# One layer of a hybrid decoder on one core: a norm's mean and two of its tiles given to other engines, and the first expert's transposes placed ahead of the loops

## Chip, cores, metric

The kernel runs on one core of a Trainium2 chip. The metric is the device time of one execution in microseconds (us), the median of several runs; less is better. The engines are named as in the profile: PE (TensorE), DVE (VectorE), ACT (ScalarE), POOL (GpSimd), SP (SyncE, which here only issues DMAs).

## What is computed

1024 tokens of width 1024, float32. The last of three sublayers is a mixture of 32 experts, top 4, and after it stands a final RMSNorm. The change lies in these two:

```
def moe_ffn(hn, ...):                       # hn = rmsnorm(h, ln_ffn)
    logits = xt @ w_router + b_router
    top_vals, top_idx = lax.top_k(logits, TOP_K); gates = softmax(top_vals)
    ... rows sorted by expert ...
    h = ragged_dot(xs, w_gate_up, sizes) + b_gate_up[e]
    act = glu * sigmoid(1.702 * glu) * (lin + 1)      # clamped
    y = (ragged_dot(act, w_down, sizes) + b_down[e]) * gates
    return segment_sum(y, tok)
...
h = h + moe_ffn(...)
return rmsnorm(h, ln_final)                 # h * rsqrt(mean(h*h) + eps) * ln_final
```

## The kernel before

Mixers, cross attention and router fill the first 1085 us of the profile. Then 32 experts ("items") run one after the other, sorted by how many rows they hold; the code exists once for each of six widths (256, 208, 184, 160, 144, 128 rows), the widest first. In this data the width of 256 holds no expert, the others hold 2, 2, 3, 6 and 19.

**The loops on PE.** For each width `up_to` nests five loops of two turns, each with an `If` on a register `at` that counts experts (L1916, L1917), and in the innermost stands `item(w)`. In it `If_lt(at, 1)` (L1909) guards `e_turn_in(0, range(4))`: the 16 transposes (L1760) that turn the first expert's gathered rows `xg`; for the 31 others they were made by the expert before. DVE copies them to `xe_t` (`x_copies`), and on that semaphore (`e_xt`) the first gate and up matmuls wait (L1376).

**The end.** All of the last expert but its own rows is summed in `d_sum` before it runs its down product. SP loads `d_sum` back as eight tiles `h_out` of 128 x 1024 (L603), and the final norm of these tiles runs beside the last matmuls:

- ACT squares and sums each tile (`squares`, L1311, semaphore `r_ss`).
- DVE makes the mean of a group of tiles (`means`, L2372, `f_mean`). The groups are F_TILES: tiles 0 and 1, tiles 2 to 5, tiles 6 and 7.
- POOL raises it to -0.5 (L1021, `f_rstd`).
- DVE multiplies a tile by its factor and by the weights `g_fin` in one instruction (`normed`, L2431), SP writes the tile to the output (L795, `f_out`).

In between DVE adds the last expert's rows (`last_rows`, two halves, `completed`, L2452), ACT squares those (L1353), DVE norms them too (`y_sb`), and POOL scatters them into the output (L1030). That scatter overwrites rows, so it waits for all eight tile writes.

ACT's last `step` has, after the squares, this loop; PE's last down product releases it piece by piece, the last piece (`e_dn[1]`, its second count) with the matmul that adds the bias (L1844):

```
for m in range(KD):
    b, k = (m // 2) % 2, m // 4 + 1
    if m % 2 == 0:
        ac.wait_ge(e_dn[b].full, 2 * i + k)
    if last:
        ...
        continue
```

Each engine carries out its own instructions in the order in which they are written.

Of the kernel before, what the change touches and what calls it, by code (L numbers as in the profile page):

```python
# [26 lines left out]
ALU = mybir.AluOpType  # L27
ACT = mybir.ActivationFunctionType
AX = mybir.AxisListType.X

P = 128
# [47 lines left out]
def build(nc, S, a, out):  # L79
    T, D, NT, KD, H, FW, E, CAP = S.T, S.D, S.NT, S.KD, S.H, S.FW, S.E, S.CAP  # L80
    ctx = ExitStack()
    with ctx:
# [38 lines left out]
        half = keep("half", [P, 16])  # L121
# [173 lines left out]
        h_out = Region(15, 47)("h_out", [P, NT, D])  # L295
        last_rows = Region(59, 63)("last_rows", [P, D])
        g_fin = r("g_fin", [P, D])
# [6 lines left out]
        rstd_f = r("rstd_f", [P, NT])  # L304
# [274 lines left out]
        s_st, r_gate = sem("s_st"), sem("r_gate")  # L579
# [3 lines left out]
        f_rstd, f_o, f_out = sem("f_rstd"), sem("f_o"), sem("f_out")  # L583
        f_mean, f_mean_done = a_latn, NT
        F_TILES = [(0, 2), (2, 6), (6, 8)]
        assert F_TILES[-1][1] == NT

        def apart(eng):
# [12 lines left out]
        def _(sp):  # L601
# [186 lines left out]
            def rows_for_norm():  # L788
                for t in range(NT):
                    load(h_out[:, t, :], d_sum[t * P:(t + 1) * P, :], f_in[t])  # L790

            def normed_rows(first):
                for t in range(NT):
                    sp.wait_ge(f_o, first + t + 1)
                    sp.dma_start(out[0, t * P:(t + 1) * P, :], h_out[:, t, :]).then_inc(f_out, 16)  # L795

            sp.wait_ge(e_left, E)
            rows_for_norm()
            normed_rows(0)

            def whole_norm():
                rows_for_norm()
                normed_rows(NT + 1)
                sp.wait_ge(f_out, 16 * 2 * NT)

            sp.wait_ge(f_out, 16 * NT)
# [4 lines left out]
        def _(po):  # L811
# [204 lines left out]
                bounds_check=T - 1, oob_is_err=False).then_inc(e_share, 16)  # L1016

            def norm_factors(first):
                for n, (t0, t1) in enumerate(F_TILES):
                    po.wait_ge(f_mean, f_mean_done + first + n + 1)  # L1020
                    po.tensor_tensor(rstd_f[:, t0:t1], rstd_f[:, t0:t1], half[:, 0:t1 - t0], ALU.pow).then_inc(f_rstd, 1)  # L1021

            norm_factors(0)
            po.wait_ge(f_mean, f_mean_done + len(F_TILES) + 1)
            po.tensor_tensor(rstd_l[:, 1:2], rstd_l[:, 1:2], half[:, 0:1], ALU.pow).then_inc(f_rstd, 1)
            further = any_further(po)
            po.wait_ge(f_out, 16 * NT)
            po.wait_ge(f_o, NT + 1)
            apart(po)
            po.indirect_dma_start(  # L1030
                out=out[0], out_offset=bass.IndirectOffsetOnAxis(ap=sidx[:, 0:1], axis=0),
# [24 lines left out]
        def _(ac):  # L1056
# [257 lines left out]
            def step(i, e, before, first=False, last=False):  # L1314
                for m in range(KD):
                    ac.wait_ge(e_glu, KD * i + m + 1)
                    ac.activation(sig[m % 2][:, :], glu[m % 2][:, :], ACT.Sigmoid, scale=1.702).then_inc(e_sig, 1)  # L1317
                    if m == 1 and before is not None:
                        rows_back(before)
                    if m == 1 and first:  # L1320
                        nothing_back()
                    if last and m >= 6:
                        squares(((0, 1), (2, 3, 4, 5, 6, 7))[m - 6], 2)
# [5 lines that stand above are left out]
                        if m % 2 == 1:  # L1329
                            ac.sem_inc(e_dn[b].free, 1)  # L1330
                        if m % 4 == 3:
                            ac.sem_inc(e_w[4 + m // 4].free, 1)
                        continue
                    x = ac.activation(y_t[:, m, :], pp2[b][:, (m % 2) * CAP:(m % 2 + 1) * CAP], ACT.Identity,  # L1334
                                      bias=b_dn[:, bass.ds(e * KD + m, 1)])
                    if m % 2 == 1:
                        x.then_inc(e_dn[b].free, 1)
                    if m % 4 == 3:
                        ac.sem_inc(e_w[4 + m // 4].free, 1)
                ac.drain().then_inc(e_yt, 1)  # L1340

            def expert_at(i):
                return ac.value_load(items[0:1, 0, bass.ds(i, 1)], min_val=0, max_val=E - 1)
# [4 lines left out]
            with ac.Fori(1, E - 1) as i:  # L1348
                step(i, expert_at(i), i - 1)
            step(E - 1, expert_at(E - 1), E - 2, last=True)  # L1350
            for b in range(2):
                ac.wait_ge(e_rows[b].free, rows_use(b, E - 1, 1) + 1)
                ac.activation(y_sb[:, 1, b * 512:(b + 1) * 512], last_rows[:, b * 512:(b + 1) * 512], ACT.Square,  # L1353
                              accum_out=sum_l[:, b:b + 1])
                ac.drain().then_inc(r_ss, 1)
# [9 lines left out]
        def _(pe):  # L1365
# [523 lines left out]
            for b in range(2):  # L1889
                pe.wait_ge(e_rows[b].free, e_rows[b].base + 1)  # L1890
                for m in range(4 * b, 4 * b + 4):
                    x = pe.transpose(wide[1][0:BP, m * P:(m + 1) * P],
                                     b_thrice[:, m, :], ident)
                x.then_inc(e_rows[b].full, 1)
            at = pe.alloc_register("item_at")
            pe.reg_mov(at, 0)
            LEVELS = 5
# [2 lines left out]
            def item(w):  # L1900
                i, n, n_before = pe.snap(at), pe.snap(held), pe.snap(held_before)
                later = pe.snap(held_later)

                def look_ahead():
                    pe.reg_mov(held_before, n)
                    pe.reg_mov(held, later)
                    pe.reg_mov(held_later, rows_in(i + 2))

                with pe.If_lt(at, 1):  # L1909
                    e_turn_in(0, range(4))  # L1910
                whole(i, i - 1, w, n_before, later, look_ahead)
                pe.reg_mov(at, i + 1)

# [21 lines left out]
        def _(ve):  # L1935
# [432 lines left out]
            def means(n, squared):  # L2368

                t0, t1 = F_TILES[n]  # L2370
                ve.wait_ge(r_ss, squared + t1)
                ve.tensor_scalar(rstd_f[:, t0:t1], sum_f[:, t0:t1], 1.0 / D, EPS, ALU.mult, ALU.add)  # L2372
                ve.drain().then_inc(f_mean, 1)
# [58 lines left out]
                ve.drain().then_inc(f_o, 1)  # L2432

            def norm(first, squared, between=None):
                for n, (t0, t1) in enumerate(F_TILES):
                    for t in range(t0, t1):
                        if between is None and t == 0:
                            means(0, squared)
                        if t == t1 - 2 and n + 1 < len(F_TILES):
                            means(n + 1, squared)  # L2440
                        ve.wait_ge(f_rstd, first + n + 1)
                        if between is not None:
                            between(t)
                        normed(h_out[:, t, :], h_out[:, t, :], rstd_f[:, t:t + 1])
# [8 lines left out]
                                        op0=ALU.mult, op1=ALU.add).then_inc(e_rows[b].free, 1)  # L2453

            def at_tile(t):
                if t == 3:
                    completed(0)
                elif t == NT - 1:
                    ve.wait_ge(r_ss, 2 * NT + 1)
                    ve.tensor_scalar(rstd_l[:, 0:1], sum_l[:, 0:1], 1.0 / D, EPS, ALU.mult, ALU.add)  # L2460
                    completed(1)
# [66 lines left out]
```

## Time and profile before

| | us |
|---|---|
| median of 3 runs | 2709.58 (2707.89 to 2711.74) |
| the profiled execution, its own time | 2707.28 |
| its span, first to last instruction | 2705.4 |
| experts, from their first matmul | from 1090.6 |
| last matmul over | 2689.2 |

The profiled execution is 2.3 us shorter than the median. A timeline row gives start, length, engine, line, operation, what is written and read, a count, and in brackets the idle time of the engine just before and what ended it.

### The profile page before, as it was taken

To read this page: it belongs to the slowest core of one execution; us is meant where nothing else is said; L and a number is where in the kernel's file an instruction comes from. 1 tells how busy PE (TensorE), PEld (TensorE's weight loads), DVE (VectorE), ACT (ScalarE), POOL (GpSimd) and SP (SyncE) were. 2 spreads that over 40 slices of the span, in tenths; PEclk is the share of its full clock that TensorE was granted. 3 is DMA by queue.
4 is the path that set the end of the run, shared out by engine and by line. 5 is a ranking of instruction groups with operands and counts; after the bars stand their busy time and mean duration, and the time that the engine had idled before them with its cause. 6 is when DMAs were issued, how large, how long until landed. Compare 5 with 4: busy or idle time off the path is not lost.

```text
span 2705.4 us, 49571 instructions
## 1 busy us (share of the span) xinstructions
PE 2638.0 (98%) x17206; PEld 2118.7 (78%) x17207; DVE 1091.5 (40%) x2701; ACT 627.4 (23%) x1386; POOL 379.9 (14%) x391
## 2 busy tenths in 40 slices
PE   9999999999999998999999999999999999999997
PEld 8455556666477774999999999998878787878785
DVE  1111145554212324433333344344455454545455
ACT  0333355553011112011111111111212121221212
POOL 0100022221000001111111111111111111112111
PEclk9999999999999998999999999999999999999998
DMA  8111243232300002765667677787888888888885
GB/s 293 47 51 54 64 151 90 79 116 92 129 1 9 31 31 103 303 209 194 221 218 254 225 276 260 269 274 264 318 299 319 301 310 306 312 297 312 300 310 202
DMA packets 108856, 533.95 MB, mean 197 GB/s; under 512 B 24290, under 2 KB 59042, under 8 KB 84208
## 3 DMA queue, kind: packets, MB, share of 16 engines
q1 hardware_dynamic: 88016, 498.99, 50.2%
q0 software_dynamic: 20768, 33.97, 5.7%
q8 instruction: 48, 0.79, 0.1%
q14 instruction: 24, 0.20, 0.0%
HBM read 506.64 MB, written 60.52 MB: 210 GB/s over the span
## 4 chain that ended last, share of the span: by engine, by line
PE 92%; DVE 3%; issue 2%; DMA 2%; ACT 1%; DVEq 1%; POOL 0%; ACTq 0%; POOLq 0%
PE bank L1376 45%; PE wide L1376 9%; PE wide L1836 9%; PE wide L1804 9%; PE bank L1426 8%; PE bank L1369 4%; PE wide L1500 2%; PE bank L1556 2%; PE bank L1760 2%; PE wide L1517 1%; DMA d_sum<-y_sb,sidx 1%; PE wide L1369 1%; DVE biased L2060 1%; DVE prob_t L2071 1%; ACT prob L1151 0%
## 5 line engine op out<-in xcount | busy, mean ns | idle before, releaser
L1376 PE MATMUL bank<-xe_t,slot 128*128 128x128 f32 (+4 forms) x8192 | 1025.2, 287 | 12.3 <-issue 11.2
L1376 PEld LDWEIGHTS bank<-xe_t,slot 128*128 128x128 f32 x8192 | 1014.5, 192 | 14.1 <-issue 13.7
L2336 DVE TENSOR_SCALAR glu<-bank,b_gu 128x256 f32<-128x256 f32 x256 | 123.8, 484 | 657.2 <-PE bank L1376 657.1
L1317 ACT ACTIVATE sig<-glu 128x256 f32<-128x256 f32 x256 | 106.7, 417 | 837.8 <-DVE glu L2336 835.5
L1836 PE MATMUL wide<-slot,act_t 128*128 128x512 f32 x608 | 267.8, 593 | 1.0 <-DVE act_t L2348 1.0
L1804 PE MATMUL wide<-act_t,slot 128*128 128x144 f32 (+3 forms) x1664 | 235.5, 302 | 0.0
L1804 PEld LDWEIGHTS wide<-act_t,slot 128*128 128x128 f32 x1664 | 231.8, 190 | 0.0
L1426 PE MATMUL bank<-w_in,xt 128*128 128x512 f32 (+1 forms) x512 | 217.6, 575 | 1.6 <-DVEq L1978 1.6
L1836 PEld LDWEIGHTS wide<-slot,act_t 128*128 128x128 f32 x608 | 112.5, 190 | 128.8 <-issue 126.2
L1334 ACT ACTIVATE y_t<-wide,b_dn 128x256 f32<-128x256 f32 x248 | 102.0, 471 | 421.2 <-PE wide L1836 212.9
L955 POOL DMA_INDIRECT xg<-d_xn,gidx x66 | 66.6, 1009 | 862.8 <-DVE gidx L2290 814.0
L1426 PEld LDWEIGHTS bank<-w_in,xt 128*128 128x128 f32 x512 | 94.8, 190 | 100.5 <-issue 100.5
L987 POOL DMA_INDIRECT share<-d_gate,sidx x64 | 67.8, 1059 | 458.6 <-DVEq L2357 415.4
L2348 DVE TENSOR_TENSOR act_t<-lin,sig 128x256 f32<-128x256 f32 x256 | 108.8, 425 | 41.0 <-issue 7.3
L1938 DVE TENSOR_TENSOR xe_t<-bank,gains 128x512 f32<-128x512 f32 x132 | 85.2, 686 | 96.8 <-PE bank L1760 91.6
L2338 DVE TENSOR_SCALAR lin<-bank,b_gu 128x256 f32<-128x256 f32 x256 | 121.6, 475 | 0.0
L2345 DVE TENSOR_TENSOR lin<-lin,glu 128x256 f32<-128x256 f32 x256 | 108.9, 425 | 19.4 <-issue 0.3
L1376 PEld LDWEIGHTS bank<-hn_t,w_xq 128*128 128x128 f32 x1024 | 115.5, 192 | 1.4 <-issue 1.1
L1376 PE MATMUL bank<-hn_t,w_xq 128*128 128x128 f32 x1024 | 115.7, 275 | 0.3 <-issue 0.3
L1376 PE MATMUL wide<-vw,px_t 128*128 128x512 f32 x256 | 112.4, 593 | 0.6 <-DVE lg_now L2171 0.6
L997 POOL DMA_INDIRECT d_sum<-y_sb,sidx x62 | 99.0, 1598 | 44.3 <-ACTq L1299 29.4
L1369 PE MATMUL bank<-const,prob 128*128 128x128 f32 x576 | 88.2, 281 | 11.6 <-DVE prob_t L2071 5.1
(302 smaller groups left out, 2455.6 us busy)
## 6 DMA issues: line engine op xcount, KB each, us to landing
slot<-in_w_gu SPq DMA_DIRECT2D x128, 2048.0 KB, 8.8
slot<-in_w_dn SPq DMA_DIRECT2D x64, 2048.0 KB, 7.7
w_in<-in_w_in SPq DMA_DIRECT2D x1, 6144.0 KB, 25.3
w_mem_k<-in_w_mem_kv SPq DMA_DIRECT2D x4, 1024.0 KB, 11.0
w_mem_v<-in_w_mem_kv SPq DMA_DIRECT2D x1, 4096.0 KB, 20.6
x_sb<-in_x SPq DMA_DIRECT2D x8, 512.0 KB, 3.3
cneg<-d_cneg SPq DMA_DIRECT2D x8, 512.0 KB, 6.6
d_vw<-mix_out SPq DMA_DIRECT2D x16, 256.0 KB, 2.2
```

The costliest lines, as they stand in the source:

```text
L997: po.indirect_dma_start(out=d_sum, out_offset=bass.IndirectOffsetOnAxis(ap=sidx[:, hb:hb + 1], axis=0), in_=y_sb[:, hb, :], in_offset=None ...
L1317: ac.activation(sig[m % 2][:, :], glu[m % 2][:, :], ACT.Sigmoid, scale=1.702).then_inc(e_sig, 1)
L1334: x = ac.activation(y_t[:, m, :], pp2[b][:, (m % 2) * CAP:(m % 2 + 1) * CAP], ACT.Identity, bias=b_dn[:, bass.ds(e * KD + m, 1)])
L1369: m = pe.transpose(dst[0:s.shape[-1], j * P:j * P + s.shape[0]], s, idn)
L1376: m = pe.matmul(dst, l, r_, start=(k == 0), stop=(k == n - 1))
L1426: m = pe.matmul(pp[b][:, 0:c1 - c0], xt[:, kk, :], w_in[:, kk, c0:c1], start=kk == 0, stop=kk == KD - 1)
L1804: x = pe.matmul(pp2[b][:, (m % 2) * CAP:(m % 2) * CAP + w], slots[4 + m // 4][:, k, (m % 4) * P:(m % 4 + 1) * P], act_t[:, k, 0:w], start= ...
L1836: x = pe.matmul(wide[1][:, hd * 512:(hd + 1) * 512], act_t[:, k, 0:P], slots[4 + hd][:, k, :], start=k == 0, stop=False)
L2336: ve.tensor_scalar(glu[b][:, :], pp[b][:, 0:CAP], b_gu[:, bass.ds(e * 2 * KD + 2 * m, 1)], 7.0, ALU.add, ALU.min).then_inc(e_glu, 1)
L2338: ve.tensor_scalar(lin[b][:, :], pp[b][:, CAP:2 * CAP], b_gu[:, bass.ds(e * 2 * KD + 2 * m + 1, 1)], 7.0, ALU.add, ALU.min).then_inc(e_gu[ ...
L2345: ve.tensor_tensor(lin[b][:, :], lin[b][:, :], glu[b][:, :], ALU.mult)
L2348: ve.tensor_tensor(act_t[:, m, :], lin[b][:, :], sig[b][:, :], ALU.mult).then_inc(e_act, 1)
```

## The change

Three things:

- The first expert's 16 transposes stand once ahead of all loops on PE; the guarded copy in each of the six widths is gone.
- In the final norm the mean of tiles 2 to 5 is made after tile 0 rather than before it, and that of tiles 6 and 7 before tile 5 rather than before tile 4.
- Tiles 2 and 3 (PO_TILES) leave DVE. ACT multiplies them by their factor (a new pair of instructions after its last `step`), POOL multiplies them by `g_fin` (`normed_here`), tile 2 between its second and third power and tile 3 after the third. The half sum `completed(0)` moves from ahead of tile 3 to ahead of tile 6. SP writes the tiles in the order 0, 1, 2, 4, 5, 3, 6, 7.

```diff
+        MEAN_AT = [0, 1, 4]
+        PO_TILES = (2, 3)
+            def shared_rows():
+                for t in (0, 1, 2, 4, 5, 3, 6, 7):
+                    if t in PO_TILES:
+                        sp.wait_ge(f_po, f_po_done + PO_TILES.index(t) + 1)
+                    else:
+                        sp.wait_ge(f_o, VE_TILES.index(t) + 1)
+                    put_rows(t)
...
+            def normed_here(t):
+                po.wait_ge(r_ex, SCALED + PO_TILES.index(t) + 1)
+                po.tensor_tensor(h_out[:, t, :], h_out[:, t, :], g_fin[:, :], ALU.mult).then_inc(f_po, 1)
+            factor(0)
+            factor(1)
+            po.wait_ge(ld["g_fin"], 32)
+            normed_here(2)
+            factor(2)
+            normed_here(3)
...
             step(E - 1, expert_at(E - 1), E - 2, last=True)
+            ac.wait_ge(f_rstd, 2)
+            for t in PO_TILES:
+                ac.activation(h_out[:, t, :], h_out[:, t, :], ACT.Copy, scale=rstd_f[:, t:t + 1]).then_inc(r_ex, 1)
...
+            e_turn_in(0, range(4))
             at = pe.alloc_register("item_at")
...
-                with pe.If_lt(at, 1):
-                    e_turn_in(0, range(4))
...
+                        if between is not None and t in PO_TILES:
+                            continue
+                        if t in means_at and (between is None or t > 0):
+                            means(means_at.index(t), squared)
...
             def at_tile(t):
-                if t == 3:
+                if t == 6:
                     completed(0)
```

ACT at the end of the last expert, before. `last_rows` is squared right after the squares of the eight tiles, and waits for the two `e_dn` semaphores of PE's down product:

```order
L1311 ACTIVATE y_sb_192,sum_f_219<-h_out_211 128x1024 [waits f_in6]
L1311 ACTIVATE y_sb_192,sum_f_219<-h_out_211 128x1024 [waits f_in7]
L1353 ACTIVATE y_sb_192,sum_l_221<-last_rows_212 128x512 [waits e_dn0_full,e_dn1_full,x_w0_free]
L1353 ACTIVATE y_sb_192,sum_l_221<-last_rows_212 128x512 [waits x_w1_free]
```

The same place now:

```order
L1340 ACTIVATE y_sb_192,sum_f_219<-h_out_211 128x1024 [waits f_in6]
L1340 ACTIVATE y_sb_192,sum_f_219<-h_out_211 128x1024 [waits f_in7]
L1382 ACTIVATE h_out_211<-h_out_211,rstd_f_220 128x1024 [waits e_dn0_full,e_dn1_full,f_rstd]
L1382 ACTIVATE h_out_211<-h_out_211,rstd_f_220 128x1024
L1385 ACTIVATE y_sb_192,sum_l_221<-last_rows_212 128x512 [waits x_w0_free]
L1385 ACTIVATE y_sb_192,sum_l_221<-last_rows_212 128x512 [waits x_w1_free]
```

The two scalings stand between, and the wait for the `e_dn` semaphores is now theirs.

POOL's norm factors, before (`a_latn` is the semaphore f_mean):

```order
L1021 TENSOR_TENSOR rstd_f_220<-rstd_f_220,half_62 128x2 [waits a_latn]
L1021 TENSOR_TENSOR rstd_f_220<-rstd_f_220,half_62 128x4 [waits a_latn]
L1021 TENSOR_TENSOR rstd_f_220<-rstd_f_220,half_62 128x2 [waits a_latn]
L1025 TENSOR_TENSOR rstd_l_222<-rstd_l_222,half_62 128x1 [waits a_latn]
```

and now:

```order
L1041 TENSOR_TENSOR rstd_f_220<-rstd_f_220,half_62 128x2 [waits a_latn]
L1041 TENSOR_TENSOR rstd_f_220<-rstd_f_220,half_62 128x4 [waits a_latn]
L1045 TENSOR_TENSOR h_out_211<-h_out_211,g_fin_213 128x1024 [waits r_ex,ld_g_fin]
L1041 TENSOR_TENSOR rstd_f_220<-rstd_f_220,half_62 128x2 [waits a_latn]
L1045 TENSOR_TENSOR h_out_211<-h_out_211,g_fin_213 128x1024 [waits r_ex]
L1054 TENSOR_TENSOR rstd_l_222<-rstd_l_222,half_62 128x1 [waits a_latn]
```

The third power, of tiles 6 and 7, now stands behind the multiplication of tile 2, which waits for ACT.

PE at the entry of the experts, now: the transposes of `xg` come first, then the loop nest, whose last row here is the wait for `e_xt` ahead of the first gate matmul.

```order
L1792 MATMUL bank1<-const_49,xg_193 128x128 [waits pt1_free]
L1792 MATMUL bank1<-const_49,xg_193 128x128 x3
L1947 UNCONDITIONAL_BRANCH
L1948 COMPARE_AND_BRANCH
...
L1934 ISA
L1822 REGISTER_ALU [waits e_xt]
```

Before, the ten branches came first and the transposes stood inside.

## Rows read from the trace of the kernel before

**Rows 1.** The page: busy time and share of the span by engine.

```profile
PE 2638.0 (98%) x17206; PEld 2118.7 (78%) x17207; DVE 1091.5 (40%) x2701; ACT 627.4 (23%) x1386; POOL 379.9 (14%) x391
```

**Rows 2.** The chain that ended last, its end: start, length, what.

```profile
2693.63 3.60 DMA out_h<-h_out
```

**Rows 3.** Timeline from 2681 to 2690, ACT and PE.

```profile
2681.52 1.06 ACT L1311 ACTIVATE y_sb<-h_out 128x1024 f32<-128x1024 f32 x1
2688.83 0.38 PE L1844 MATMUL wide<-b_rows,this_b 96*128 96x256 bf16 x2
2689.38 0.63 ACT L1353 ACTIVATE y_sb<-last_rows 128x512 f32<-128x512 f32 x1 [6.71 <-PE wide L1844]
```

**Rows 4.** Timeline of DVE from 2680 to 2694.

```profile
2680.31 0.17 DVE L2372 TENSOR_SCALAR rstd_f<-sum_f 128x4 f32<-128x4 f32 x1 [2.20 <-ACTq L1312]
2680.61 4.10 DVE L2431 SCALAR_TENSOR_TENSOR h_out<-h_out,rstd_f,g_fin 128x1024 f32<-128x1024 f32 x3
...
2687.28 4.09 DVE L2431 SCALAR_TENSOR_TENSOR h_out<-h_out,rstd_f,g_fin 128x1024 f32<-128x1024 f32 x3
2691.56 0.15 DVE L2460 TENSOR_SCALAR rstd_l<-sum_l 128x1 f32<-128x1 f32 x1 [0.19 <-issue]
2691.64 0.74 DVE L2452 SCALAR_TENSOR_TENSOR last_rows<-wide,share,last_rows 128x512 f32<-128x512 f32 x1
2692.29 1.28 DVE L2431 SCALAR_TENSOR_TENSOR h_out<-h_out,rstd_f,g_fin 128x1024 f32<-128x1024 f32 x1
```

**Rows 5.** Timeline of POOL from 2687 to 2700.

```profile
2687.27 0.70 POOL L1021 TENSOR_TENSOR rstd_f<-rstd_f,half 128x2 f32<-128x2 f32 x1 [5.66 <-DVEq L2373]
...
2698.20 1.06 POOL L1030 DMA_INDIRECT out_h<-y_sb,sidx  x1 [3.63 <-DMA out_h<-h_out]
```

**Rows 6.** Groups by line and form, elsewhere in the kernel: busy us, mean ns of one.

```profile
L1234 ACT ACTIVATE rn<-h_res,rstd 128x1024 f32<-128x1024 f32 x2 | 2.3, 1148 | 3.4 <-POOL rstd L933 3.4
...
L883 POOL TENSOR_TENSOR w_o<-w_o,gains 128x1024 f32<-128x1024 f32 x8 | 14.9, 1892 | 16.8 <-DMA w_o<-in_w_o 16.5 <-issue 0.3
L870 POOL TENSOR_TENSOR o_t<-o_t,rr_all 128x1024 f32 x6 | 14.1, 2355 | 42.6 <-DMA rr_all<-d_rr 42.6
```

**Rows 7.** DMA over the last 30 us: queue issues; then one microsecond by the windows view.

```profile
out_h<-h_out SPq DMA_DIRECT2D x8, 512.0 KB, 3.4
...
2683.00:2684.00 1.00, 1.00 (x3) 0.40 (x3) 0.88 (x2) 0.00 (x0) 0.00 (x0) 1.00 1.03 414
```

**Rows 8.** Timeline of DVE and POOL, windows ending at 1095 and 1093.6.

```profile
1073.90 2.67 DVE L2281 TENSOR_SCALAR hot<-const,shift,key 128x256 bf16<-128x256 f32 x8 [1.13 <-issue]
...
1090.39 2.12 POOL L977 TENSOR_TENSOR b_fp<-b_fp,b_mid 96x1024 f32<-96x1024 f32 x1
...
1091.19 2.63 DVE L2281 TENSOR_SCALAR hot<-const,shift,key 128x256 bf16<-128x256 f32 x2 [0.86 <-issue]
```

**Rows 9.** Timeline of PE: the entry of the experts, two changes of width, one change of expert.

```profile
1078.29 1.92 PE L1892 MATMUL wide<-const,b_thrice 128*96 128x128 f32 x8 [0.89 <-issue]
1085.76 3.84 PE L1760 MATMUL bank<-const,xg 128*128 128x128 f32 x16 [5.55 <-DMA xg<-d_xn,gidx]
1090.61 13.17 PE L1376 MATMUL bank<-xe_t,slot 128*128 128x208 f32 x64 [1.01 <-DVEq L2305]
...
1236.15 11.91 PE L1376 MATMUL bank<-xe_t,slot 128*128 128x184 f32 x64 [2.39 <-issue]
...
1301.71 10.14 PE L1376 MATMUL bank<-xe_t,slot 128*128 128x184 f32 x64
...
1540.37 9.78 PE L1376 MATMUL bank<-xe_t,slot 128*128 128x144 f32 x64 [3.28 <-issue]
```

**Rows 10.** Windows of 1 us; the third last column is the granted clock as a share.

```profile
1238.00:1239.00 1.00, 1.00 (x5) 1.00 (x4) 0.00 (x0) 0.00 (x0) 0.00 (x0) 0.50 0.88 377
1093.00:1094.00 1.00, 1.00 (x5) 0.97 (x4) 1.00 (x2) 0.00 (x0) 0.67 (x1) 0.50 1.00 426
1094.00:1095.00 1.00, 1.00 (x8) 1.00 (x6) 1.00 (x4) 0.00 (x0) 0.00 (x0) 1.00 0.95 410
```

More of the change, by code:

```diff
@@ L585, in build @@
         F_TILES = [(0, 2), (2, 6), (6, 8)]
+        MEAN_AT = [0, 1, 4]
+        PO_TILES = (2, 3)
+        VE_TILES = [t for t in range(NT) if t not in PO_TILES]
+        f_po, f_po_done = r_gate, 1
+        SCALED = 4
         assert F_TILES[-1][1] == NT
@@ L790, in rows_for_norm, with put_rows @@
                     load(h_out[:, t, :], d_sum[t * P:(t + 1) * P, :], f_in[t])
+            def put_rows(t):
+                sp.dma_start(out[0, t * P:(t + 1) * P, :], h_out[:, t, :]).then_inc(f_out, 16)
+            def shared_rows():
[5 more added lines that the diff above has]
+                    put_rows(t)
             def normed_rows(first):
@@ L794, in normed_rows @@
                     sp.wait_ge(f_o, first + t + 1)
-                    sp.dma_start(out[0, t * P:(t + 1) * P, :], h_out[:, t, :]).then_inc(f_out, 16)
+                    put_rows(t)
             sp.wait_ge(e_left, E)
             rows_for_norm()
-            normed_rows(0)
+            shared_rows()
             def whole_norm():
                 rows_for_norm()
-                normed_rows(NT + 1)
+                normed_rows(len(VE_TILES) + 1)
                 sp.wait_ge(f_out, 16 * 2 * NT)
@@ L1018, in norm_factors, with factor @@
             def norm_factors(first):
[L1019 to L1023, printed above, removed]
+                for n in range(len(F_TILES)):
+                    factor(n, first)
+            def factor(n, first=0):
+                t0, t1 = F_TILES[n]
+                po.wait_ge(f_mean, f_mean_done + first + n + 1)
+                po.tensor_tensor(rstd_f[:, t0:t1], rstd_f[:, t0:t1], half[:, 0:t1 - t0], ALU.pow).then_inc(f_rstd, 1)
+            def normed_here(t):
[7 more added lines that the diff above has]
+            normed_here(3)
             po.wait_ge(f_mean, f_mean_done + len(F_TILES) + 1)
@@ L1027, in _ @@
             po.wait_ge(f_out, 16 * NT)
-            po.wait_ge(f_o, NT + 1)
+            po.wait_ge(f_o, len(VE_TILES) + 1)
             apart(po)
@@ L2434, in norm @@
             def norm(first, squared, between=None):
+                means_at = MEAN_AT if between is None else [0, 1, 5]
                 for n, (t0, t1) in enumerate(F_TILES):
                     for t in range(t0, t1):
[L2437 to L2440, printed above, removed]
+                        if between is not None and t in PO_TILES:
+                            continue
+                        if t in means_at and (between is None or t > 0):
+                            means(means_at.index(t), squared)
                         ve.wait_ge(f_rstd, first + n + 1)
```

## The prediction

> **What bounds the kernel now.** I read the shares of busy time first: PE 98%, so away from PE's work only its few gaps and what lies outside it can be won or lost [rows 1]. The change touches two such places: the stretch after PE's last matmul, over at 2689.2 [rows 3], and PE's way from expert to expert. I then read the end of the chain of waits and the timelines of the last 25 us. Of the 16 us behind PE's last matmul, the chain shows DVE's tile 7, ending at 2693.57 [rows 4], then 3.60 us for its write to land [rows 2]. Only then, at 2697.23, does POOL issue the scatter of the last rows [rows 5], and that takes to the end of the span at 2705.4, 8.2 us which the change leaves alone. So what counts in the end is when the last of eight tile writes lands. Why is DVE late? It waits for squares until 2680.31 and starts its tiles there [rows 4]; eight tiles at 1.40 us start to start, two half sums and two means then fill it to 2693.57. The change lifts two tiles off that load. The question is what the two that stay behind it, 6 and 7, then wait for.
>
> **ACT's scalings start late.** ACT ends its last square of a tile at 2682.67 (2681.52 and 1.06, then the read of the accumulator), is idle for 6.71 us and squares the last rows at 2689.38, released by PE's bias matmul [rows 3]. That instruction in fact stands behind the loop over `e_dn` in ACT's last step, and the wait belongs to the place, not to the instruction: in the new order the scaling of tile 2 carries it. So it starts at 2689.38 too, although its factor needs only the squares that are there by 2680.31 [rows 4]. A multiplication by a factor of this size takes ACT 1.15 us [rows 6]: 2690.5.
>
> **POOL stands behind it.** POOL's multiplication of tile 2 by the weights has no row. Its bounds are two groups of 128x1024: 1.89 us with a broadcast second operand, 2.36 with two full ones [rows 6]. Here both are full: 2.36, to 2692.9. The factor of tiles 6 and 7 is queued behind it on POOL; before it was made at 2687.27 in 0.70 us [rows 5], now it is ready at 2693.6 to 2693.7. DVE waits for it ahead of the half sum `completed(0)` and tile 6, and ACT's square of that half waits for DVE. DVE, done with tiles 0, 1, 4, 5 by about 2685, idles for some 8.7 us.
>
> **DVE from 2693.7.** The half sum takes 0.65 to the next start (2691.64 to 2692.29), tile 6 1.28, and from the mean at 2691.56 to the end of tile 7 were 2.0 us [rows 4]. With 0.2 between: 2693.7 + 0.65 + 1.3 + 0.2 + 2.0 = 2697.85, against 2693.57, **4.3 us later** if nothing else interferes. That is the low end.
>
> Something may: POOL's multiplication of tile 3 begins in the very moment when DVE is released. Eight of DVE's instructions of one form took 2.67 us; two of them took 2.63 while POOL was busy with a two-operand instruction from 1090.39 to 1092.51 and with the one after it [rows 8]. DVE was held until POOL was through. If so here, tile 6 waits until 2693.7 + 2.36 = 2696.1, ends at 2697.4, and tile 7 at 2697.4 + 0.2 + 2.0 = 2699.6, **6.0 us later**. The Trainium skill says the same (SBUF — State Buffer, Who interferes with whom): the two engines share a port pair as an exclusive lock, and a VectorE instruction with two SBUF inputs contends with a GpSimd one. The held rows had another form (one tensor input), so no run here shows that this form is held; by the page it would be.
>
> **The writes.** SP's queue holds the same trap: the writes of tiles 4 and 5, ready long before, stand behind tile 2's wait at 2692.9. Six of eight writes then come at once. One takes 3.4 us from issue to landing; at a full rate of 414 GB/s its 0.524 MB occupy the DMA engines for 1.27 us [rows 7]. 2692.9 + 3.4 + 5 x 1.27 = 2702.7, against 2697.23: **5.5 us later**, whatever DVE does. With the held tile 6 it is DVE that is last: 2699.6 + 3.6 = 2703.2, 6.0 later. I take 5.8 for the tail, between these two, bounds 4.3 and 6.0 (the low one if several writes overlap better than this). The last rows' own path (a mean, a power of 0.6, 1.3 on DVE) ends near 2702 and stays hidden behind the writes by about 1 us. The means that moved win nothing: tile 0 starts some 2 us earlier, but DVE is idle later.
>
> **PE, change of width.** From expert to expert of one width PE shows no gap, the row at 1301.71 has none [rows 9]: a branch less there is worth nothing. At the four changes of width PE idles 2.39 to 3.28 us waiting for nothing but its own instructions [rows 9]. I count some 24 branches of the loops on that way, and one of them goes. 2.39 / 24 is 0.1 us; if PE's queue covers some 5.6 us more of it (my estimate from the pace of matmuls, 32 at 0.17), it is 0.37. Four times: -0.4 to -1.5; I take -0.8.
>
> **PE, entry of the experts.** Before, the loop nest was walked between 1080.2 (end of the row at 1078.29) and 1085.76, under 5.55 us of waiting for the gather [rows 9]. Now the wait for the gather comes first and the nest after it. It can only be hidden between the transposes' issue and the release of the first gate matmul at 1090.61. Some 16 branches at 0.1 to 0.37 us are 1.6 to 5.9 us. Starting at 1086.3, if PE's sequencer runs ahead of its transposes, they end at 1092.2 at the latest; starting at 1088.8, if it is held by the third and fourth transposes' waits, at 1090.4 to 1094.7. Cost: 0 to 4.1 us, I take +1.0. The Trainium skill (Runtime: NRT & Kernel Launch, Instruction fetch mechanics) adds that a taken branch to code not yet on the engine forces a fetch before it can go on. The first width, 256, is jumped over whole, and that fetch was hidden before as well. A fetch has no row of its own length, so the sum leaves it inside the 4.1.
>
> **The clock.** After the entry the granted clock stands at 0.50, the level of 1.2 GHz, until 1094.0, and at one change of width too, at 1238 [rows 10]. The first 64 matmuls of that expert took 11.91 us, those of the next 10.14 [rows 9]: 1.77 us per fall. Two of the four changes show this (184 and 144 rows). Whether a gap is followed by a fall is nothing that I can tell from its length, so this term is 0, with +-3.5 as the noise of an execution.
>
> **The sum.** +5.8 - 0.8 + 1.0 = +6.0. Against the profiled execution, 2707.28, this is 2713.3; the median lies 2.3 higher, and to it the forecast is 2709.58 + 6.0 = **2715.6**. About 0.2%, 5.4 us, is what a measurement can tell from no change: slower is above 2715.0, faster below 2704.2. The forecast lies just above that edge.
>
> **Rivals.**
> 1. The tail costs only DVE's and POOL's own time, tile 6 is not held and writes overlap: +4.3 - 0.8, entry free. 2713.1, within 0.2%. For it: no row shows this pair of instructions collide, nor six writes at once. Against it: DVE was held by POOL [rows 8], and one write already brings the DMA share to 1.03 [rows 7]. Chance 0.22.
> 2. The loop nest behind the transposes is as long as its upper bound and the low clock lasts one stretch longer: +5.8 - 0.8 + 4.1 + 1.77 = +10.9: 2720.5. For it: gaps of 3 us with nothing else in them. Chance 0.20.
> 3. It does what it says: ACT's scalings run right after its squares at 2682.7. Then tile 2 is ready at 2683.8 + 2.4 = 2686.2, the third power at 2686.9, `completed(0)` and tile 6 by 2689, and tile 7 follows the last matmul: 2689.2 + 0.1 + 2.0 = 2691.3, 2.3 us earlier. 2709.58 - 2.3 - 0.8 = 2706.5, not slower. It decides by one point: ACT would have to pass the `e_dn` loop before about 2686. The 6.71 us in rows 3 speak against it. Chance 0.05.
>
> The forecast (+5 to +7.5) has the remaining 0.53. Slower: two thirds of the forecast's, with noise, nearly all of rival 2 and little of rival 1, together 0.57. Within 0.2%: 0.40. Faster: 0.03. The range runs from 2712.0, rival 1 with a little luck of the clock, to 2719.5, most of rival 2.
>
> **What would show it.** In the changed profile: ACT's first scaling at 2689.4 relative to PE's last matmul, released by PE; POOL's multiplication 2.4 us long; DVE idle for over 8 us before the half sum; tile 6 starting when POOL's second multiplication ends (held) or 0.65 after the half sum (not held); the last tile write landing 14 us after PE's end instead of 8; PE's idle time before the first gate matmul above 1.0 us; at the changes of width gaps shorter by 0.1 to 0.4. I am wrong if ACT scales before 2688, or if POOL's multiplication stays under 1.5 us.

## The result, and the profile after

The changed kernel takes 2716.97 us (median of 7 runs, 2715.17 to 2720.53) against 2707.89 (7 runs, 2705.17 to 2711.74) for the kernel before: a ratio of 1.0033, 95% interval 1.0024 to 1.0042. It is slower by about 9 us. The forecast was 2715.6, in a range of 2712.0 to 2719.5, with slower as the likeliest case. It was built on a median of 2709.58 for the kernel before, which in these runs is 1.7 us lower: as a difference the forecast was +6.0, and +9.1 was measured.

The profiled execution took 2716.51, its span is 2714.7 (before: 2707.28 and 2705.4). The span is 9.3 us longer, and the two places of the forecast hold all of it. PE's last bias matmul begins at 2692.42 instead of 2688.83 [rows 3], 3.6 later; from there to the end of the span it was 16.6 us and is now 22.3, 5.7 more.

The end first. Timeline of the changed kernel, all engines (start, length, engine, line, operation; idle time before and what ended it):

```profile
2692.42 0.39 PE L1876 MATMUL wide<-b_rows,this_b 96*128 96x256 bf16 x2
2692.97 2.19 ACT L1382 ACTIVATE h_out<-h_out,rstd_f 128x1024 f32<-128x1024 f32 x2 [6.70 <-PE wide L1876]
2694.26 2.34 POOL L1045 TENSOR_TENSOR h_out<-h_out,g_fin 128x1024 f32<-128x1024 f32 x1 [9.15 <-ACT h_out L1382]
2696.56 0.69 POOL L1041 TENSOR_TENSOR rstd_f<-rstd_f,half 128x2 f32<-128x2 f32 x1
2697.23 2.34 POOL L1045 TENSOR_TENSOR h_out<-h_out,g_fin 128x1024 f32<-128x1024 f32 x1
2697.29 0.75 DVE L2484 SCALAR_TENSOR_TENSOR last_rows<-wide,share,last_rows 128x512 f32<-128x512 f32 x1 [8.79 <-POOL rstd_f L1041]
2697.96 2.69 DVE L2462 SCALAR_TENSOR_TENSOR h_out<-h_out,rstd_f,g_fin 128x1024 f32<-128x1024 f32 x1
...
2701.57 1.28 DVE L2462 SCALAR_TENSOR_TENSOR h_out<-h_out,rstd_f,g_fin 128x1024 f32<-128x1024 f32 x1
```

Read it downwards; what ended each idle time is a row further up. ACT's idle time of 6.70 us, once ahead of the square of the last rows [rows 3], now stands ahead of the two scalings. POOL waits for ACT, DVE for POOL's power, 8.79 us. Tile 6 on DVE is 2.69 us long where such a row was 1.28 [rows 4]. Then the chain goes to the write of tile 7, released at 2702.90:

```profile
2702.90 2.97 DMA out_h<-h_out
```

It lands 13.5 us after PE's last matmul began, 8.4 before [rows 2]: 5.1 us later. The rest of the 5.7 lies behind it, in the scatter of the last rows: from this landing to the end of the span it is 8.8 us, 8.2 before. The DMA view of the last stretch has the scatter's time to landing, kernel before and changed kernel:

```profile
out_h<-y_sb,sidx POOLq DMA_INDIRECT x1, 3.3
```
```profile
out_h<-y_sb,sidx POOLq DMA_INDIRECT x1, 4.0
```

Now the entry of the experts and the four changes of width, the same kernel, timeline of PE:

```profile
1085.61 3.87 PE L1792 MATMUL bank<-const,xg 128*128 128x128 f32 x16 [5.43 <-DMA xg<-d_xn,gidx]
1097.48 12.94 PE L1408 MATMUL bank<-xe_t,slot 128*128 128x208 f32 x64 [8.01 <-issue]
```
```profile
1242.43 11.91 PE L1408 MATMUL bank<-xe_t,slot 128*128 128x184 f32 x64 [2.05 <-issue]
1374.39 8.96 PE L1408 MATMUL bank<-xe_t,slot 128*128 128x160 f32 x64 [2.45 <-issue]
1545.73 8.10 PE L1408 MATMUL bank<-xe_t,slot 128*128 128x144 f32 x64 [2.77 <-issue]
1853.20 7.41 PE L1408 MATMUL bank<-xe_t,slot 128*128 128x128 f32 x64 [2.36 <-issue]
```

The first gate matmul starts at 1097.48, before at 1090.61 [rows 9]: 6.9 us later, behind 8.01 us in which PE waits for nothing that the profile shows. The four gaps are 2.05, 2.45, 2.77 and 2.36, together 1.6 us shorter than the 2.39, 2.87, 3.28 and 2.70 of before. And behind the third the clock did not fall: its 64 matmuls took 8.10 us instead of 9.78, 1.7 us less. 6.9 - 1.6 - 1.7 = 3.6, which is PE's shift.

The 1.7 us look like luck of one execution, but the profiles of the runs below speak against it. In all seven without any guard in the widths, with gaps of 9.6 to 9.7 us in all (the changed kernel and six others), the clock fell at one of the four changes. In all seven with a guard, inside the loops or ahead of them, with gaps of 10.8 to 11.3 us in all (the kernel before and six others), it fell at two. Which of the four it was does not go by the length of the gap: it fell after 2.05 us and did not after 2.77. So the missing fall probably belongs to the change. There is one profile for each kernel, and no run shows why.

### The profile page after: what moved, and what is told of

Its sections match the earlier page's. It is cut to its first block, busy times and chain, and to the rows that moved or that the text cites. A ratio compares the mean times of both kernels' runs of the same rounds, so it can differ in the third digit from the quotient of the medians.

```text
span 2714.7 us, 49508 instructions
## 1 busy us (share of the span) xinstructions
PE 2636.2 (97%) x17206; PEld 2117.4 (78%) x17207; DVE 1091.3 (40%) x2699; ACT 629.5 (23%) x1388; POOL 384.6 (14%) x393
## 4 chain that ended last, share of the span: by engine, by line
PE 92%; DVE 2%; issue 2%; DMA 2%; ACT 1%; DVEq 1%; POOL 0%; ACTq 0%; POOLq 0%
PE bank L1408 45%; PE wide L1868 9%; PE wide L1408 9%; PE wide L1836 9%; PE bank L1458 8%; PE bank L1401 4%; PE wide L1532 2%; PE bank L1588 2%; PE bank L1792 2%; PE wide L1549 1%; DMA d_sum<-y_sb,sidx 1%; PE wide L1401 1%; DVE biased L2091 1%; DVE prob_t L2102 0%; ACT prob L1180 0%
## 6 DMA issues: line engine op xcount, KB each, us to landing
w_mem_k<-in_w_mem_kv SPq DMA_DIRECT2D x4, 1024.0 KB, 10.9
```

## The experiments

Where a span's end is given "behind PE", it is counted from the start of PE's last bias matmul: 16.6 us before, 22.3 in the changed kernel. That leaves out what the entry and the clock did.

### Each half of the change alone

```diff
# kernel before
+            e_turn_in(0, range(4))
             at = pe.alloc_register("item_at")
...
-                with pe.If_lt(at, 1):
-                    e_turn_in(0, range(4))
```

> The kernel before with the first expert's transposes ahead of the loops and nothing else. My theory (the parts add up): the entry loses 6.9 us on PE, as in the changed kernel (idle 8.0 us before the first gate matmul at about 1097.5), the four changes of width give back 1.6, the end is as before; with the clock's falls at +-1.8 each, +3.5 to +5.5 us against the kernel before. Rival (the entry's 8 us belong to something else in the changed kernel, such as a fetch that fell badly because of other code): idle of about 1 to 4 us and a time within 2 us of the kernel before.

2712.5 us, ratio 1.0018 (1.0008 to 1.0028). Timeline of PE:

```profile
1088.78 3.87 PE L1760 MATMUL bank<-const,xg 128*128 128x128 f32 x16 [5.48 <-DMA xg<-d_xn,gidx]
1101.25 13.23 PE L1376 MATMUL bank<-xe_t,slot 128*128 128x208 f32 x64 [8.60 <-issue]
```

8.60 us idle, the gaps 2.05 to 2.78, and an end 16.6 us behind PE, as before. The loss at the entry needs nothing of the new tail.

The other half is the changed kernel with PE's code of before:

```diff
# changed kernel
-            e_turn_in(0, range(4))
...
+                with pe.If_lt(at, 1):
+                    e_turn_in(0, range(4))
```

> The changed kernel with PE's code as before (guarded transposes in each width): the final norm's change alone. My theory: +5.7 us, all of it after PE's last matmul: ACT's first scaling 0.5 us after PE's bias matmul, tile 6 on DVE 2.7 us long. Rival (the end of the changed kernel is later because PE's part shifted something): +1 to +3 us.

2714.73 us, ratio 1.0027 (1.0017 to 1.0037). Its span ends 22.4 us behind PE, 5.8 more than before; PE's entry and gaps are those of before. DVE's tile 6:

```profile
2694.73 2.69 DVE L2463 SCALAR_TENSOR_TENSOR h_out<-h_out,rstd_f,g_fin 128x1024 f32<-128x1024 f32 x1
```

The tail's loss stands by itself. The two halves add up to 0.45% where the whole measured 0.33; the intervals of 0.1 each allow it. The trace's terms are the better account: 5.8 for the tail and 5.3 for entry and gaps (6.9 - 1.6), less 1.7 for the clock, are 9.4, against the 9.3 of the whole.

### Only the means moved

```diff
# kernel before
+                means_at = [0, 1, 5]
...
-                        if between is None and t == 0:
-                            means(0, squared)
-                        if t == t1 - 2 and n + 1 < len(F_TILES):
-                            means(n + 1, squared)
+                        if t in means_at and (between is None or t > 0):
+                            means(means_at.index(t), squared)
```

> The kernel before with the two means moved and nothing else: no tile leaves DVE, PE as before. My theory: tile 0 starts about 2 us earlier in DVE's idle time, DVE's load after that is unchanged, so tile 7 ends 1.4 us earlier (one tile's time) and the kernel is 1.0 to 1.5 us faster. Rival (PE's last matmul bounds the end, or the writes do): no difference, within 0.3 us at the end by the trace.

2708.12 us, ratio 1.000 (0.999 to 1.001): no difference that the times show. The trace shows one. Timeline, PE and DVE's tile 7:

```profile
2688.69 0.38 PE L1844 MATMUL wide<-b_rows,this_b 96*128 96x256 bf16 x2
...
2690.81 1.28 DVE L2431 SCALAR_TENSOR_TENSOR h_out<-h_out,rstd_f,g_fin 128x1024 f32<-128x1024 f32 x1
```

Tile 7 ends 3.4 us behind PE instead of 4.7, and the span 15.3 instead of 16.6. My statement in the forecast that the moved means win nothing held only for the changed kernel, where DVE idles later. Alone they give 1.3 us by the trace, half a thousandth, below what these runs can tell.

### ACT's place, POOL's place

First ACT: the scalings right after its squares, ahead of the `e_dn` loop.

```diff
# changed kernel
                     if last and m >= 6:
                         squares(((0, 1), (2, 3, 4, 5, 6, 7))[m - 6], 2)
+                if last:
+                    ac.wait_ge(f_rstd, 2)
+                    for t in PO_TILES:
+                        ac.activation(h_out[:, t, :], ..., ACT.Copy, scale=rstd_f[:, t:t + 1]).then_inc(r_ex, 1)
```

> The changed kernel with ACT's two scalings moved from behind its last step to right after its squares, ahead of the waits for PE's down product. Counted from the start of PE's last bias matmul, the span ended 16.6 us later before and 22.3 us later in the changed kernel. My theory (ACT's place in its own queue is the cause): the scalings run about 6 us before that matmul, POOL's first multiplication about 4.8 us before it, tile 7 ends 3.5 to 4 us after it instead of 10.4, the span 15.5 to 16 us after it. Rival (POOL's own time and the shared writes are the cost): the end is still 19 us or more behind PE.

One run, 2710.55 us. Timeline:

```profile
2684.43 2.19 ACT L1356 ACTIVATE h_out<-h_out,rstd_f 128x1024 f32<-128x1024 f32 x2
...
2685.72 3.04 POOL L1045 TENSOR_TENSOR h_out<-h_out,g_fin 128x1024 f32<-128x1024 f32 x1 [2.54 <-ACT h_out L1356]
...
2690.12 2.69 DVE L2463 SCALAR_TENSOR_TENSOR h_out<-h_out,rstd_f,g_fin 128x1024 f32<-128x1024 f32 x1
2690.49 0.38 PE L1877 MATMUL wide<-b_rows,this_b 96*128 96x256 bf16 x2
```

ACT's place is the cause of most of it: the scalings run 6 us ahead of PE's last matmul, tile 7 ends 4.5 us behind PE (10.4 in the changed kernel), the span 18.2. But I expected 15.5 to 16. Both multi-input instructions are stretched, POOL's to 3.04 and DVE's to 2.69, and the chain's last write takes longer than any before:

```profile
2695.07 4.87 DMA out_h<-h_out
```

The measured 18.2 lies between my theory and its rival (19 or more): 1.6 us of the loss survive the mending of ACT. Then POOL: its third power first, ACT still late.

```diff
# changed kernel
-            normed_here(2)
             factor(2)
+            normed_here(2)
             normed_here(3)
```

> The changed kernel with POOL's third power ahead of its first multiplication; ACT's scalings stay late. DVE then has the factor for tile 6 some 9 us earlier. My theory: tile 6 is done before PE's last matmul, and tile 7 about 8 us after its start instead of 10.4 (it now waits for ACT's square of the first half sum, behind the two scalings, and for POOL's second multiplication). The six writes then start when tile 2 is ready, 4.2 us after, and take turns: the last lands no earlier than 13 to 14 us after it, so the end moves by less than 0.5 us. Rival (writes overlap freely): last landing at 11.3 us, the kernel 2 us faster than the changed one.

One run, 2716.75 us. Tile 7 is ready 7.5 us behind PE, three us earlier than in the changed kernel, and the last write lands at 13.7, no earlier than its 13.5. The timeline of POOL and DVE and the chain's last write:

```profile
2694.15 4.65 POOL L1045 TENSOR_TENSOR h_out<-h_out,g_fin 128x1024 f32<-128x1024 f32 x2 [5.15 <-ACT h_out L1382]
...
2696.57 3.30 DVE L2462 SCALAR_TENSOR_TENSOR h_out<-h_out,rstd_f,g_fin 128x1024 f32<-128x1024 f32 x1
```
```profile
2700.68 5.43 DMA out_h<-h_out
```

Rival refuted: six writes that start together take turns. In the changed kernel too the DMA engines are full for nearly 8 us, as its windows show (last columns: DMA share, GB/s), at both ends of that stretch:

```profile
2698.00:2699.00 1.00, 0.00 (x0) 0.00 (x0) 1.00 (x2) 0.72 (x2) 1.00 (x1) 0.50 1.02 410
...
2704.00:2705.00 1.00, 0.00 (x0) 0.00 (x0) 1.00 (x1) 0.00 (x0) 0.00 (x0) 0.50 1.02 418
```

### Does POOL hold DVE?

```diff
# changed kernel
             factor(2)
+            po.wait_ge(f_o, len(VE_TILES))
             normed_here(3)
```

> The changed kernel with a wait ahead of POOL's second multiplication, until DVE has ended tile 7. Theory A (POOL's multiplication holds DVE's scalar_tensor_tensor, which shows as 2.69 us for tile 6): tile 6 takes 1.28 us, tile 7 ends 1.4 us earlier, 9.0 us after the start of PE's last bias matmul. Theory B (tile 6 was long for another reason): still 2.69. The kernel as a whole gets slower, since tile 3 and the two writes behind it come later.

One run, 2723.04 us. Tile 6, with POOL kept quiet:

```profile
2700.67 1.27 DVE L2463 SCALAR_TENSOR_TENSOR h_out<-h_out,rstd_f,g_fin 128x1024 f32<-128x1024 f32 x1
```

1.27 us instead of 2.69, and tile 7 ends 9.0 us behind PE as expected. The extra 1.4 us is POOL's multiplication. This is the form of instruction that rows 8 lacked. The Trainium skill says that a VectorE instruction with two SBUF inputs contends with a GpSimd one that reads SBUF (SBUF — State Buffer, Who interferes with whom). This trace agrees, and from both sides: in the run with ACT early it is POOL that is held by DVE's tile 5 (3.04 instead of 2.34).

### What PE waits for at the entry

The transposes behind the loops of the empty width 256, correct for this data alone:

```diff
# changed kernel
-            e_turn_in(0, range(4))
...
             for c, w in enumerate(reversed(WIDTHS)):
+                if c == 1:
+                    e_turn_in(0, range(4))
                 up_to(below[c], w, LEVELS)
```

> The changed kernel with the transposes placed after the loops of the empty width 256 and ahead of those of width 208, correct for this data. Theory A (the jump over the unused code of width 256 and what it has to fetch is most of the 8.0 us of PE's idle time): the jump is hidden again under the wait for the gather, and idle before the first gate matmul falls to 2 to 3 us, as at a change of width. Theory B (each branch of the nest costs the same, about 0.5 us for 16 of them): the ten branches that stay behind the transposes leave 5 us.

One run, 2713.35 us. PE's first gate matmul:

```profile
1093.74 13.36 PE L1408 MATMUL bank<-xe_t,slot 128*128 128x208 f32 x64 [1.01 <-DVEq L2337]
```

The idle time is 1.01, as before the change, not the 2 to 3 that I expected under theory A: here the ten branches of width 208's own nest hide entirely behind the transposes. Theory B, and with it my price of a branch, falls. The 7 us come from having the way across the code of width 256 behind the transposes. The rest of the change on PE does pay: from its transposes to the first matmul of the last width this profile needs 761.0 us, the kernel before 764.3, which is the gaps' 1.6 and the clock's 1.7. Is it the number of jumps?

```diff
# changed kernel
+                if c == 0:
+                    with pe.If_lt(at, below[c]):
+                        up_to(below[c], w, LEVELS)
```

> The changed kernel with the loops of the empty width 256 inside one more If, so that their code is jumped over once, instead of twice with a jump back in between (two turns of the outermost loop). In the run with the transposes behind this width PE's idle time before the first gate matmul had fallen from 8.0 to 1.0 us, so the way over this code is the cost. Theory A (each jump over 1000 instructions costs by itself): idle falls from 8.0 to some 4 us. Theory B (the code beyond has to be brought in once, however often it is jumped to): idle stays within 1 us of 8.0.

One run, 2720.89 us. PE's first gate matmul:

```profile
1099.78 14.13 PE L1408 MATMUL bank<-xe_t,slot 128*128 128x208 f32 x64 [6.91 <-issue]
```

6.91 us idle instead of 8.01. One jump forward costs nearly what two and one back do. It took 1.1 less, a little more than B allowed. The five profiles with the changed kernel's PE code lie between 7.95 and 8.60, so the repetition counts for something, but most is paid once: B.

What is paid once is most likely a fetch of instructions. The records of the DMA queue q8 show blocks of instructions (number, MB, share, in the half microsecond from the time that is named). I take them for PE's, because they move when only PE's code does: with the entry alone changed they come from 1096.0 and 1102.0, with the tail alone changed from 1081.0 and 1084.0. Kernel before, from 1080.5 and from 1084.0:

```profile
q8 instruction: 1, 0.02, 12.2%
```
```profile
q8 instruction: 1, 0.02, 15.7%
```

Changed kernel, from 1092.5 (the next one comes from 1098.5):

```profile
q8 instruction: 1, 0.02, 12.0%
```

Before, a block was there 2.7 us after PE had begun its last work ahead of the nest (1078.29). I read it as the first one past the jump. In the changed kernel PE's transposes are free to go at 1085.61, and it came 7 us later. In between SP starts five loads of 2 MB each; its timeline in the changed kernel:

```profile
1086.52 2.54 SPq L608 DMA_DIRECT2D slot<-in_w_gu  x3
1089.25 0.89 SPq L608 DMA_DIRECT2D slot<-in_w_dn  x2
```

They wait for the very gather for which PE's transposes wait. So by moving the fetch behind that wait the change puts it among 10 MB of weights. The Trainium skill (Runtime: NRT & Kernel Launch, Instruction fetch mechanics) states that a taken branch to code not yet on the engine forces a fetch before it can go on; the 8.01 us of idle time at this jump fit that.

Do the loads make it slow? One thing speaks for it: the two blocks at the entry lie 3.0 to 3.5 us apart in the profiles with the jump ahead of the wait (the kernel before, the new tail alone, the moved means alone, the transposes behind width 256), and 6.0 us apart in all six with the jump among the loads. Two things speak against a simple account. The stretch before the change was not quiet; the DMA share and GB/s (last two columns) in the microsecond just ahead of the block of 1080.5:

```profile
1079.00:1080.00 1.00, 1.00 (x6) 0.75 (x4) 0.84 (x3) 0.59 (x1) 1.00 (x1) 0.50 0.99 426
```

An earlier load of 2 MB filled the engines then, and from 1081 to 1084 the gather kept them at 0.60 to 0.93. And in the changed kernel 5.0 us pass between the block of 1092.5 and the first gate matmul. The ten branches of the nest lie in that stretch too, where nothing hides them, and no view says how it divides.

### Can the good parts be had alone?

Three kernels with the guarded transposes once per width, ahead of its loops:

```diff
# kernel before
-                with pe.If_lt(at, 1):
-                    e_turn_in(0, range(4))
...
             for c, w in enumerate(reversed(WIDTHS)):
+                with pe.If_lt(at, 1):
+                    with pe.If_lt(at, below[c]):
+                        e_turn_in(0, range(4))
                 up_to(below[c], w, LEVELS)
```

> The kernel before with PE's guarded transposes taken out of the six widths and put, once per width and still guarded (first expert, and this width holds an expert), ahead of that width's loops. So the empty width 256 is passed before the wait for the gather. My theory: PE's idle time before the first gate matmul 1.0 us as before, the four changes of width 1.2 to 1.7 us shorter in all; with the clock's falls 0 to 4 us faster, some 1.6 on average. Rival (an If taken before the loops costs as much as the one inside saved): no difference in the idle rows.

2713.44 us, ratio 1.0011 (1.0000 to 1.0023). It is not faster, and the terms are wrong. The idle time ahead of the first gate matmul is 1.01, as expected, but only because the wait now stands ahead of the transposes. The gaps at the changes of width shrank by 0.4 us in all (2.31, 2.83, 3.04, 2.63), not 1.2 to 1.7, although the If is gone from them as well; another If stands in their way now. And PE's timeline at the entry:

```profile
1096.34 3.69 PE L1760 MATMUL bank<-const,xg 128*128 128x128 f32 x16 [14.82 <-issue]
```

14.82 us idle, though the rows `xg` were there around 1087: 9.4 us more than the gather takes. There are blocks in q8 from 1082.0, 1085.0 and 1085.5, ahead of the loads, which SP starts at 1087.93, and one from 1093.0 among them, 7.5 us after the one before it:

```profile
q8 instruction: 1, 0.02, 11.6%
```

The runs of this kernel fall in two groups: three from 2701.24 to 2707.9, nine from 2711.16 to 2717.72. The one with the means moved as well:

> The same with the two means moved as well, no tile leaving DVE. Expected: the idle rows of PE as in the run with the guard alone, and the span 15.3 us after the start of PE's last bias matmul instead of 16.6, as in the run with the means alone: 2.5 to 3 us faster than the kernel before by the terms, 0.1%. Rival: the end is bound by the writes and gives nothing.

2712.13 us, ratio 1.0007 (0.9998 to 1.0016); 14.57 us idle at the entry, end 15.4 us behind PE; three runs below 2707.1, eight from 2710.9. So the idle rows and the end came as expected, the 2.5 to 3 us did not. With tile 7 ahead of the second half sum:

```diff
+            completed(1)
+            ve.wait_ge(r_ss, 2 * NT + 1)
+            ve.tensor_scalar(rstd_l[:, 0:1], sum_l[:, 0:1], 1.0 / D, EPS, ALU.mult, ALU.add)
+            ve.drain()
```

(and the same lines gone from ahead of tile 7)

> The same again, with tile 7 normed ahead of the second half sum and ahead of the wait for ACT's square of the first. Expected: tile 7 ends 2.4 us after the start of PE's last bias matmul instead of 3.4, its write lands at 6.0, the last rows are normed at 6.3 and now end the chain; the span ends 14.5 us after it. 3.5 to 4 us faster than the kernel before by the terms. Rival (the second half sum, one tile later now, makes the last rows later than the writes were): 15.3 as before this edit.

2713.29 us, ratio 1.001 (1.000 to 1.002). Tile 7 ends 2.4 us behind PE as expected, but its write takes longer for it and lands at 7.0, not 6.0; the span ends at 15.8, and nothing is won over 15.4 (five runs up to 2708.83, seven from 2712.72):

```profile
2699.82 4.51 DMA out_h<-h_out
```

And last the changed kernel with the faults that I had found in its tail mended (ACT early, factor first, writes in the order 0, 1, 4, 5, 2, 3, 6, 7) and the guard per width:

> The changed kernel with all of its tail's faults mended: ACT's scalings ahead of the waits for PE, POOL's third power ahead of its multiplications, the ready writes of tiles 4 and 5 ahead of tile 2's, and the guard per width on PE. It tells what sharing two tiles with POOL is worth at its best. Theory (DVE and POOL hold each other, so a tile costs 2.35 us of the shared time on POOL against 1.28 on DVE and nothing is won): span end 15.5 to 16.8 us after PE's last bias matmul, against 15.3 with the means alone and all tiles on DVE. Rival (the load taken off DVE counts): 14 us or less.

One run, 2708.65 us. Its span ends 17.5 us behind PE: worse than the 15.3 of the kernel that leaves all tiles on DVE, worse than the 16.6 of before, and outside my 15.5 to 16.8. POOL's and DVE's rows, and the write that ends the chain:

```profile
2685.86 5.63 POOL L1045 TENSOR_TENSOR h_out<-h_out,g_fin 128x1024 f32<-128x1024 f32 x2
...
2686.59 2.70 DVE L2465 SCALAR_TENSOR_TENSOR h_out<-h_out,rstd_f,g_fin 128x1024 f32<-128x1024 f32 x1
```
```profile
2692.72 5.12 DMA out_h<-h_out
```

Tile 6 is held (2.70), POOL's pair is too (5.63 instead of 2 x 2.34), and tile 7 ends 3.4 us behind PE, exactly as with all tiles on DVE: nothing was gained there. The 2.2 us lost against that run lie behind tile 7. Its write takes 5.12 instead of 3.67, with POOL's tile 3 ready only 1.2 us ahead of it, and the scatter behind it takes 9.0 instead of 8.2. At the entry this kernel has the same PE code as the three above and shows the short wait:

```profile
1085.68 3.87 PE L1793 MATMUL bank<-const,xg 128*128 128x128 f32 x16 [5.31 <-DMA xg<-d_xn,gidx]
```

Its blocks in q8 came from 1079.5, 1081.0 and 1084.0, all ahead of the loads at 1086.60. One code for PE, two outcomes, apart by 9 us at the entry. In the short one the last block comes before the loads. In the long one there are five blocks from 1074 to 1093 instead of three, the last of them among the loads; why there are more, no run shows. No kernel here is measurably faster than the one before.

## Why the prediction was right, point by point

- **ACT's scalings start late: right.** Forecast 0.5 us after the last bias matmul begins, released by PE; measured 0.55 (2692.97). Moving them early gave back 4.1 of the 5.7 us.
- **POOL behind ACT, DVE behind POOL: right.** Multiplication 2.36 forecast, 2.34 measured; DVE's wait "some 8.7", 8.79.
- **Tile 6 held: right,** taken from another form of instruction, and shown for this one by keeping POOL quiet.
- **The writes: right in kind.** They would have bound the end without the holding too; the run with the factor first shows it (tile 7 three us earlier, no gain). The last landing was forecast 5.5 to 6.0 later and came 5.1 later.
- **The tail as a whole: +5.8 forecast, +5.7 measured, in part by luck.** I held the 8.2 us from the last landing to the end fixed, and they were 8.8. That miss and the landing's cancel. With the tail alone it is +5.8.
- **Change of width: the size was off.** -0.8 forecast in bounds of -0.4 to -1.5; measured -1.6 in the gaps, 0.34 to 0.51 each. The removed guard was worth more than one branch out of 24 by my division.
- **Entry of the experts: this is the step that failed.** I gave +1.0, at most +4.1; measured +6.9 and, alone, 7.6 in idle time. The term priced sixteen branches. With the transposes behind width 256 the sixteen fell to ten and the whole loss was gone. What costs is the way across unused code, most of it paid once, which fits one fetch. I had named the fetch and left it inside the 4.1, because "that fetch was hidden before as well"; I did not ask what would start in the same moment as the wait behind which it was moved. SP's queue, which I followed at the tail, I did not follow there.
- **The clock: a term put at nothing that was not nothing.** It was -1.7 in the profile. I could not tell from a gap's length whether a fall follows, and that holds; but the number of falls goes with the guard in all 14 profiles, one fall without any guard, two with one. A fall costs 1.67 us where the same matmuls can be compared; I had 1.77.
- **The sum.** +5.8 - 0.8 + 1.0 = +6.0 was forecast; the profile has +5.7 - 1.6 + 6.9 - 1.7 = +9.3, the medians +9.1. That lies above the forecast's own band of +5 to +7.5. The time itself, 2716.97, came within 1.4 us of 2715.6 because three things took from the entry's miss of 5.9: the gaps, the clock, and a median of the kernel before that was 1.7 us lower than the one I built on. That is luck.
- **Which rival came closest:** the second, a loop nest dearer than its bound, at +10.9. It had the right place and the wrong mechanism.

What stays open: shown is that the way across the code of width 256, put behind the wait for the gather, costs the 7 us. That it is a fetch, and that the loads delay it, is read from when the blocks come, from their spacing and from the two groups of runs. No run took the loads away, so a crossing that nothing hides might cost as much without them.

## What to carry to other kernels

When work is moved to an idle engine, look at what stands ahead of it in that engine's queue: ACT was idle for 6.7 us at the right time, but the idle time lay ahead of a wait that the new work inherited, and POOL passed the delay on to DVE. When a wait is moved ahead of other work, ask what else it releases in the same moment; here the way over unused code went from under the wait to behind it, into the first microseconds of 10 MB of loads. And sharing elementwise work with two full operands between DVE and POOL can be worth nothing even in the best order tried: 2.34 us of POOL against 1.28 of DVE, during which the other may stand still.

## What the runs showed of the hardware that I had not expected

- A way of PE across about 1000 unused instructions stayed hidden in 5.5 us of other waiting, and cost 6.9 to 8.6 us of PE's idle time behind that wait, when it met five loads of 2 MB. In three profiles with the way ahead of the wait, the last block of instructions still fell among the loads, and PE stood idle for up to 14.8 us, 5.4 of them the gather's. The 1000 are an estimate: one expert of 208 rows shows 421 matmuls and 422 weight loads from 1090.6 to 1163.0, and waits and branches come on top.
- Writes of 0.5 MB landed in 2.6 to 3.9 us when DVE paced them. Where they piled up behind tile 2 it was up to 4.4 (changed kernel), 5.5 (factor first) and 5.8 (ACT early), at 397 to 418 GB/s in the changed kernel.
- The holding goes both ways: DVE's 1.28 us instruction became 2.69 to 3.30, POOL's 2.34 became 3.04, and POOL's power of two columns 1.78 instead of 0.69 beside DVE's tile 5.
